# Delta rule of a two-block model: key products and M three units ahead, neighbouring units' work between the dependent products, and no identity products

## The reference, cut to what matters

```
gc = cumsum(g);  decay[i,j] = exp(gc_i - gc_j) for i >= j
m    = strict_lower((k*beta) @ k.T * decay)         # "M"
tmat = inverse(I + m)                               # triangular
u    = tmat @ (v*beta);  w = tmat @ (k*beta*exp(gc))
qk   = (q @ k.T) * decay
# over the chunks, with a state s (64 x 64 per head):
v_new = u - w @ s
o     = (q*exp(gc)) @ s + qk @ v_new
s     = s * g_last + k_dec.T @ v_new
```

## Time and profile before

| | us |
|---|---|
| median of 3 runs (lowest, highest) | 3595.54 (3592.28, 3597.2) |
| the profiled execution: its own time | 3594.88 |
| its span, first to last instruction | 3593.1 |
| PE busy in the span | 3366.4 (94%) |
| PE weight loads busy | 2497.4 (70%) |
| DVE, ACT, POOL busy | 1653.8, 1210.2, 1035.1 |
| first transpose of unit 0 in `gdn`, first product of the next stage | 1772.03, 2095.78 |

### The profile page before, as it was taken

How to read it: one execution, slowest core, us unless ns; L and a number is a source line. 1 busy time by engine, 2 the same in 40 slices (tenths; PEclk the granted TensorE clock), 3 DMA queues, 4 the chain that set the end, 5 groups by cost and what they waited for, 6 DMA issues and landing times.

```text
span 3593.1 us, 43314 instructions
## 1 busy us (share of the span) xinstructions
PE 3366.4 (94%) x17748; PEld 2497.4 (70%) x17748; DVE 1653.8 (46%) x3116; ACT 1210.2 (34%) x2188; POOL 1035.1 (29%) x894
## 2 busy tenths in 40 slices
PE   7999999888899999989799998999999998999998
PEld 3346888655788865645588866888887547848886
DVE  7744446598466666224455524112224117721213
ACT  2413333347323336135422214212213226733222
POOL 0233444460344410021244402222222022014443
PEclk9999999999999999999999899999999999999999
DMA  7424555210355541100111111111111112012222
GB/s 295 186 93 153 209 200 199 88 47 1 117 200 209 213 181 47 46 27 1 33 47 38 29 60 46 71 70 49 71 69 49 53 38 74 1 47 94 95 104 83
DMA packets 67621, 335.56 MB, mean 93 GB/s; under 512 B 32416, under 2 KB 35424, under 8 KB 42592
## 3 DMA queue, kind: packets, MB, share of 16 engines
q1 hardware_dynamic: 66560, 330.56, 24.6%
q10 hardware_dynamic: 864, 2.24, 0.2%
HBM read 325.86 MB, written 6.91 MB: 93 GB/s over the span
## 4 chain that ended last, share of the span: by engine, by line
PE 77%; DVE 11%; ACT 5%; DMA 2%; POOL 2%; issue 2%; SPq 1%; POOLq 0%; DVEq 0%; ACTq 0%
PE PSB L557 15%; PE PSB L649 14%; PE PSB L653 14%; PE PSB L650 14%; PE PSB L1235 2%; PE PSB L1257 2%; PE PSB L1244 2%; PE PSB L3006 1%; DVE SB L390 1%; DMA SB<-in_ada 1%; PE PSB L1796 1%; DVE SB L1329 1%; DVE SB L1640 1%; DVE SB L1345 1%; DVE SB L1638 1%
## 5 line engine op out<-in xcount | busy, mean ns | idle before, releaser
L653 PE MATMUL PSB<-R,WSR 128*128 128x512 f32 x2556 | 871.9, 371 | 0.0
L557 PE MATMUL PSB<-SB 128*128 128x512 f32 x1760 | 655.2, 534 | 11.8 <-ACT SB L1455 9.2
L623 POOL TENSOR_TENSOR WSR<-SB,ahead 128x1024 fp32r<-128x1024 f32 x164 | 393.1, 2397 | 672.8 <-ACT ahead L592 672.8
L557 PEld LDWEIGHTS PSB<-SB 128*128 128x128 f32 x1760 | 338.8, 193 | 325.6 <-issue 299.5
L649 PE MATMUL PSB<-R,ahead 128*128 128x512 f32 x1528 | 561.9, 368 | 0.0
L650 PE MATMUL PSB<-R,ahead 128*128 128x512 f32 x1528 | 546.1, 367 | 0.0
L653 PEld LDWEIGHTS PSB<-R,WSR 128*128 128x128 f32 x2556 | 449.6, 189 | 64.1
L623 POOL TENSOR_TENSOR WSR<-SB,ffn_weights 128x1024 fp32r<-128x1024 f32 x96 | 230.2, 2398 | 389.9 <-ACT ffn_weights L592 389.9
L649 PEld LDWEIGHTS PSB<-R,ahead 128*128 128x128 f32 x1528 | 286.9, 188 | 63.1
L649 PE MATMUL PSB<-R,ffn_weights 128*128 128x512 f32 x868 | 324.4, 374 | 6.3 <-POOL WSR L623 6.2
L650 PEld LDWEIGHTS PSB<-R,ahead 128*128 128x128 f32 x1528 | 287.0, 188 | 48.3
(11 more groups left out here) (377 smaller groups left out, 4839.7 us busy)
## 6 DMA issues: line engine op xcount, KB each, us to landing
SB<-in_w SPq DMA_DIRECT2D x95, 2048.0 KB, 8.2
SB<-in_ada SPq DMA_DIRECT2D x96, 1024.0 KB, 5.2
SB<-gate_rows SPq DMA_DIRECT2D x12, 512.0 KB, 3.9
SB<-in_rpb SPq DMA_DIRECT2D x8, 448.0 KB, 3.6
spill<-SB SPq DMA_DIRECT2D x1, 3072.0 KB, 9.6
SB<-gate_rows SPq DMA_DIRECT2D x24, 128.0 KB, 3.8
SB<-spill SPq DMA_DIRECT2D x1, 3072.0 KB, 11.5
SB<-in_x SPq DMA_DIRECT2D x8, 256.0 KB, 6.5
```

What stands on the lines that cost most here:

```text
L557: ins = e.mm(banks[ring[(g + c) % len(ring)]][0:m, 0:n], t[:, 0:m], xs[k][:, lo:lo + n], k == 0, k == nkt - 1)
L623: e.tt(lr, t, hf, ALU.subtract).then_inc(*G.up(("lo", j)))
L653: ins = e.mm(b[:, 0:n], wl, xh[:, lo:lo + n], False, last)
```

## The change

- The identity products are gone: every count in `BUSY` is 0.
- `kk` and the decay are made three units ahead (`kk(n + 3)`, `decay(n + 3)`, `products(n + 3)`). M and the decay get a third buffer. Its place is one of the two slots of the weight panels; the panel that was loaded into it early is now loaded near the end of the stage, after level 6's first product of unit 9.
- s and o of unit n - 1 move from the end of unit n - 1 to just behind the transposes of unit n (for units 9 and later they stay at the end of the unit). The tokens, `kq` and the DVE work on them are for unit n + 1 in place of n + 2, and stand between the levels; so do both parts of `past`. `carried` now stands behind `products` on DVE.
- SP issues `blocks_sp(n + 3)` ahead of `inverse_sp(n + 2)`. POOL clears DT for n + 1, inverts n + 2, then adds the output of n - 1, then takes the past off the values of n + 1.

```diff
-BUSY = {("y", 4): 4, ("d", 4): 2, ("y", 5): 2, ("d", 5): 4, ("y", 6): 5, ("u", 6): 1}
+BUSY = {("y", 4): lambda n: 0, ("d", 4): lambda n: 0,
+        ("y", 5): lambda n: 0, ("d", 5): lambda n: 0,
+        ("y", 6): lambda n: 0, ("u", 6): lambda n: 0}
 FF2 = ((0, 4), (4, 8), (8, 12), (12, 16), (16, 19), (19, 22))
...
-            MTd, DMd, DTd = ([XREG[:, i * 2048 + d * 1024:i * 2048 + (d + 1) * 1024] for d in range(2)] for i in range(3))
-            DM, DT, MT = ([a[d][:, y * 512:(y + 1) * 512] for d in range(2) for y in range(2)] for a in (DMd, DTd, MTd))
-            dec = lambda n: DECAY[n % 2]
+            late = W.where["e_out", 0, 0] // PANEL
+            spare = wslot[(late + 1) % NSLOT]
+            MTn, DMd, DTd = ([XREG[:, i * 2048 + d * 1024:i * 2048 + (d + 1) * 1024] for d in range(2)] for i in range(3))
+            MTn = [spare[:, 0:1024]] + MTn
+            DECAY = [spare[:, 1024:2048]] + DECAY
+            DM, DT = ([a[d][:, y * 512:(y + 1) * 512] for d in range(2) for y in range(2)] for a in (DMd, DTd))
+            mt_of = lambda n: MTn[n % 3]
+            dec = lambda n: DECAY[n % 3]
...
+                if 1 <= n < 10:
+                    use(n - 1, "s"), use(n - 1, "o")
+                use(n, "y", 0, 4), use(n, "y", 1, 4)
+                if 1 <= n < 11:
+                    use(n + 1, "vq", 0)
+                use(n, "d", 0, 4), use(n, "d", 1, 4)
+                use_front(n + 1, ("tok", 0), ("tok", 1))
+                use(n, "y", 0, 5), use(n, "y", 1, 5)
+                use(n, "t", 0, 4), use(n, "t", 1, 4)
+                if n == 11:
+                    use("out", 4)
+                use_front(n + 1, ("kq", 0), ("kq", 1))
+                use(n, "d", 0, 5), use(n, "d", 1, 5)
+                if 1 <= n < 11:
+                    use(n + 1, "vq", 1)
+                use(n, "y", 0, 6), use(n, "y", 1, 6)
+                use_front(n + 3, ("kk", 0), ("kk", 1))
...
             def front_sp(e):
 
-                panels(e, "e_out", 0, 0)
                 e.wait_ge(rows_out, 32)
                 e.wait_ge(*mst.at("q_turn", 7))
+                e.wait_ge(*mst.at("panel", late - 1))
                 gates_in(e, 0)
-                e.wait_ge(*mst.at("score", 35))
                 gates_in(e, 1)
+                gates_in(e, 2)
                 blocks_sp(e, 0)
                 inverse_sp(e, 0)
 
             def sp(e):
                 after(e, st)
-                for n in range(12):
-                    if n < 10:
-                        gates_in(e, n + 2)
-                    if n < 11:
-                        blocks_sp(e, n + 1)
-                        inverse_sp(e, n + 1)
+                blocks_sp(e, 1)
+                gates_in(e, 3)
+                inverse_sp(e, 1)
+                blocks_sp(e, 2)
+                for n in range(10):
+                    if n < 8:
+                        gates_in(e, n + 4)
+                    if n < 9:
+                        blocks_sp(e, n + 3)
+                    inverse_sp(e, n + 2)
+                e.wait_ge(*st.at("md", 9, 1, 6))
+                e.wait_ge(*st.at("at", 9, 1))
+                panels(e, "e_out", 0, 0)
 
             def gates_in(e, n):
                 d, c, cl, j0 = chunk(n)
                 u = 2 * c + d
                 if n >= 2:
-                    e.wait_ge(*st.at("at", n - 2, 1))
-                    e.wait_ge(*st.at("mt", n - 2, 1))
+                    e.wait_ge(*st.at("kk", n - 2, 1))
+                if n >= 3:
+                    e.wait_ge(*st.at("at", n - 3, 1))
+                    e.wait_ge(*st.at("mt", n - 3, 1))
...
+                    if 1 <= n < 10:
+                        state(n - 1)
+                        out_of(n - 1)
...
                     doubled(4)
                     past(n + 1, 0)
                     corrected(4)
-                    past(n + 1, 1)
+                    tokens(n + 1, 0), tokens(n + 1, 1)
                     doubled(5)
                     turned(4)
                     if n == 11:
                         out(4)
+                    kq(n + 1)
                     corrected(5)
+                    past(n + 1, 1)
                     for y in range(2):
...
-                    kk(n + 2)
+                    kk(n + 3)
                     turned(5)
...
-                    kq(n + 2)
-                    tokens(n + 2, 0)
+                    if n == 9:
+                        state(n)
                     if n == 11:
                         out(2), out(1)
-                    e.wait_ge(*st.at("u", n))
-                    if n < 10:
-                        free(e, n, "s")
-                        e.wait_ge(*st.at("kd", n))
-                        for h in range(8):
-                            e.mm(bank(n, "s")[par(h % 2), col(h // 2, 64)], KD[d][:, col(h, 64)], U[d][:, col(h, 64)]).then_inc(*P.up(("s_sum", n)))
-                    free(e, n, "o")
-                    e.wait_ge(*st.at("at", n, 0))
-                    e.wait_ge(*st.at("at", n, 1))
-                    for h in range(8):
-                        e.mm(bank(n, "o")[:, col(h, 64)], AT[d][:, col(h)], U[d][:, col(h, 64)]).then_inc(*P.up(("o_sum", n)))
-                    tokens(n + 2, 1)
+                    if n >= 9:
+                        out_of(n)
...
+                    if 1 <= n < 10:
+                        state(n - 1)
+                    decay_arg(n + 3)
...
-                        if lv == 5:
-                            carried(n + 1)
+                        if lv == 5 and n < 11:
+                            values(n + 1), keys(n + 1)
+                        if lv == 4 and 1 <= n < 10:
+                            out_of(n - 1)
...
-                    products(n + 2, 0)
-                    products(n + 2, 1)
+                    scores(n + 1, 0), scores(n + 1, 1)
+                    products(n + 3, 0), products(n + 3, 1)
+                    carried(n + 1)
...
+                def added(n):
+                    c = chunk(n)[1]
+                    e.wait_ge(*st.at("o", n))
+                    e.wait_ge(*st.at("o_zero", c))
+                    if n:
+                        e.wait_ge(*st.at("o_added", n - 1))
+                    e.tt(O[c], O[c], TQ[n % 2], ALU.add).then_inc(*G.up(("o_added", n)))
+
+                cleared_pool(e, 1)
+                inverse(1)
                 for n in range(12):
-                    d, c, cl, j0 = chunk(n)
-                    inverse(n + 1)
+                    d = n % 2
+                    if n:
+                        cleared_pool(e, n + 1)
+                    inverse(n + 2)
+                    if 1 <= n < 10:
+                        added(n - 1)
                     if 1 <= n < 11:
                         e.wait_ge(*st.at("past", n + 1))
                         e.wait_ge(*st.at("vb", n + 1))
                         e.tt(VB[1 - d], VB[1 - d], U[1 - d], ALU.subtract).then_inc(*G.up(("rest", n + 1)))
-                    e.wait_ge(*st.at("o", n))
-                    e.wait_ge(*st.at("o_zero", c))
-                    if n:
-                        e.wait_ge(*st.at("o_added", n - 1))
-                    e.tt(O[c], O[c], TQ[d], ALU.add).then_inc(*G.up(("o_added", n)))
+                    if n >= 9:
+                        added(n)
```

More of the change, by code:

```diff
@@ L2032, in mla, with first_out @@
             tb = att.tbanks
+            def first_out(tile_):
+                return min(NSLOT, W.where["e_out", 0, 0] // PANEL + 1 - W.where[tile_] // PANEL)
             def sp(e):
@@ L2397, in pe, with out_of, state @@
                 after(e, st)
-                for n in range(2):
-                    if n:
-                        kk(n)
-                    kq(n), tokens(n, 0), tokens(n, 1)
+                def out_of(n):
+                    d = n % 2
+                    free(e, n, "o")
+                    e.wait_ge(*st.at("u", n))
+                    e.wait_ge(*st.at("at", n, 0))
+                    e.wait_ge(*st.at("at", n, 1))
+                    for h in range(8):
+                        e.mm(bank(n, "o")[:, col(h, 64)], AT[d][:, col(h)], U[d][:, col(h, 64)]).then_inc(*P.up(("o_sum", n)))
+                def state(n):
+                    d = n % 2
+                    free(e, n, "s")
+                    e.wait_ge(*st.at("u", n))
+                    e.wait_ge(*st.at("kd", n))
+                    for h in range(8):
+                        e.mm(bank(n, "s")[par(h % 2), col(h // 2, 64)], KD[d][:, col(h, 64)], U[d][:, col(h, 64)]).then_inc(*P.up(("s_sum", n)))
+                kk(1)
+                kq(0), tokens(0, 0), tokens(0, 1)
+                kk(2)
                 for n in range(12):
@@ L2665, in dve, with state, out_of @@
                     v.memset(SS[d], 0.0).then_inc(*D.up())
-                for n in range(2):
-                    if n:
-                        products(n, 0), products(n, 1)
-                    scores(n, 0), keys(n), scores(n, 1), values(n)
+                def state(n):
+                    d, c, cl, j0 = chunk(n)
```

(43 more changed lines are left out.)

70 lines of the change are left out of this document (32 added, 38 removed).

## The result

| | before | changed |
|---|---|---|
| median of 20 runs (lowest, highest), us | 3597.51 (3590.91, 3604.38) | 3606.40 (3597.94, 3618.39) |
| profiled execution: its own time, span | 3594.88, 3593.1 | 3600.53, 3598.7 |
| mean granted clock of that execution | 0.973 | 0.961 |
| T0 to T2, T2 to T10, T10 to the end of the stage, us | 54.0, 212.2, 57.5 | 59.9, 207.3, 60.0 |

The account below looks back on a forecast made before the run. Two rounds of about 25.8 us a unit, SP-POOL-transfers and PE, were taken to bind. Units -27.7, start +5 and +1.5, end -1, clock +12 gave -10.2: profiled 3584.7, median 3585.4; range 3571 to 3605.

Parts of the forecast that it names:

- the one of a unit at full clock: Sign of being right: transposes 22 to 24 us apart in units 2 to 8 where PEclk is 1.0.
- one of being wrong: Sign of being wrong: the first product of the next stage starts no earlier than 2095.8.
- a unit without a fall: PE's dependent steps in one steady unit at full clock: sum 22.8 us against 25.8, bounds 22.3 and 24.
- T2 to T10 without falls: From unit 2's transposes to unit 10's, before clock losses: 184.5 us, 27.7 less than before.
- falls in these eight units: PE's clock drops in units 2 to 9: four at 3 us each, +12, bounds +0 and +35.
- start, to T2: Up to unit 2's transposes: +5 from POOL's two inverses before added(0), +1.5 from low clock; bounds +1 and +10.
- units 10 and 11: Stage's last two units: chains of waits, -1 together for identity products at low clock; bounds -2.5 and +2.
- the price of a fall: Cost of one clock drop behind level 6: 3 us, against 4.4 read from unit 7 of the kernel before.
- The slower one: Rival: the clock falls in every unit, eight falls costing 35 us, +13 in all, 3608; chance 0.15.
- The first rival: Rival: the clock falls no more often than before, so the 12 goes: -22, 3573; chance 0.24.
- POOL as the bound of every unit: Rival: added behind the inverse holds up carried in every unit, units back at 25.8: +2, 3597; chance 0.14.
- the one weighed ahead: Skill's rule on PE's clock: avoid long idle gaps between bursts; by it alone no steady unit would fall.

Follow-up runs that it names:

- e2: Changed kernel with three identity products a unit, only in level 6: one ahead of its second product, two ahead of u; 3587.08 us, ratio 0.9973.
- e5: e2 with the start mended: unit 3's decay taken up later in unit 0, POOL adding output n - 1 before inverse n + 2; 3576.70 us, 0.9941.
- e10: e2 with only POOL's order changed: output of n - 1 added ahead of the inverse of n + 2; 3576.12 us, ratio 0.9937.
- e6: e5 with the identity product counts of the kernel before put back ahead of the levels in units 10 and 11; 3578.01 us, 0.9943.
- e3: Kernel before with all 18 identity products a unit taken out, nothing else changed; 3650.28 us, ratio 1.0151.
- e11: Kernel before with 8 identity products a unit, in level 6 alone (5, 1 and 2), those of levels 4 and 5 gone; 3600.82 us, 1.0005.
- e12: e8 with keys(n + 1) on DVE behind level 4's subtraction in place of behind level 5's mask; 3562.36 us, ratio 0.9901.
- e7: Changed kernel with three identity products a unit, ahead of level 4's second and both of level 5's products; 3608.00 us, ratio 1.0030.
- e8: e6 with kk(n + 3) moved between level 6's second product and u, replacing identity products there in units 0 to 8; 3571.07 us, 0.9925.
- e9: e2 with only the decay of unit 3 taken up later in unit 0; 3586.44 us, ratio 0.9974.

## Why the prediction was wrong

The forecast was 3585.4; the measured 3606.4 is just above the range's 3605. Of the signs named ahead, the one of a unit at full clock came (22.8 us), and so did one of being wrong: the next stage's first product starts at 2101.2, no earlier than 2095.8. In the profiled execution, step by step:

| step | predicted | measured |
|---|---|---|
| a unit without a fall | 22.8 | 22.8 (e2, e5) |
| T2 to T10 without falls | 184.5 | 184.6 (e5), 184.5 (e10) |
| falls in these eight units | 4 x 3 = 12 | 4 x 5.7 = 22.8 |
| start, to T2 | +5 +1.5 | +5.9 |
| units 10 and 11 | -1 | +2.5 |
| the stage | -10.2 | +3.4 |

**The failed step** is the price of a fall: "I expect four in the eight units from 2 to 9, at 3 us each, fewer than 4.4 because kq and tokens no longer stand in the slow stretch". The number of falls was right, but by luck: no step of the prediction gives four and not some other number. Each took 5.7 us: two units next to each other are 23.9 + 27.4 = 51.3 for 2 x 22.8 = 45.6. Two things made 3 of it.

First, the old price was read too low. I took 4.4 from unit 7 alone, but the low stretch goes on into unit 8, whose row and first two PE rows are these (kernel before; warm they take 1.04 and 1.13):

```profile
1986.00:2012.60 26.60, 25.84 (x327) 23.66 (x326) 15.02 (x25) 7.04 (x17) 12.31 (x35) 0.93 0.19 42
```

```profile
1986.02 1.91 PE L2411 MATMUL PSB<-SB 128*128 128x128 f32 x8
1987.73 1.91 PE L2417 MATMUL PSB<-SB 128*128 128x128 f32 x8
```

Both units together are 30.2 + 26.6 = 56.8 us for 2 x 25.8 = 51.6: the fall cost 5.2, nearly what one costs in the new order. Second, I took 1.4 off for the steps that leave the slow stretch, as if the stretch ended with them. It lasted about 14 us in both kernels, so what leaves is replaced by what comes next, and here that is the chain itself. The prediction priced u, o and the transposes (0.6, 1.8 and 0.9 by its rows; 1.09, 1.68 and 0.88 came); s, level 4's two products and the key part of `past` stood in the slow stretch too and took 0.43, 0.83, 0.45 and 0.92 more. Of the 2.7 us by which the price was short, 0.8 is the reading of unit 7 alone, 1.4 is what I took off and 0.5 is the new order. 22.8 for 12 is 10.8 of the 13.6 us by which the stage missed.

**The rest of the stage.** The end explains another 3.5; the start gives back 0.6. The end's term was argued from identity products at low clock, and e6 shows that they had no say there.

**From the stage to the medians.** Of the 8.9 us, the profiled executions show 5.65: 3.4 in this stage, 2.0 ahead of it and 0.2 behind it. Ahead of it a difference of 2.3 is there already at the first head's projection, where nothing was changed and which differs from execution to execution. The other 3.2 lie in executions without a trace. Their mean granted clocks are listed: of the changed kernel's 20 runs, the fastest (3597.94) has 0.963, the three slowest (3616.93 to 3618.39) 0.957, 0.954 and 0.956; the profiled one, at 3600.53, has 0.961 and is the third fastest. That the clock falls more often in the slower ones is what these numbers fit; no trace shows where.

**The rivals.** The slower one had the right mechanism, the clock, and its 3608 is near the result, but for another reason than its sum: not eight falls at 4.4 from a sixth on, but four at 5.7, a later end, and what the untraced executions add. The first rival (no more falls, 3573) is nearest to e10 and e5, 3576.1 and 3576.7, but these have the start mended as well; e2, with the start as it was, came to 3587.1. POOL as the bound of every unit did not come: SP's waits for POOL are gone, and units at full clock take 22.8. Its +2 does not come out of the prediction's own numbers either: eight units of 25.8, +6.5 and -1 make -0.3.

**The start** came out as sized, 5.9 us for 6.5, but not as told, and that is luck too. I had put a gap of about 10 us on PE in unit 1, ended by the last subtraction. In the changed kernel's profile unit 1 has no PE gap over 0.67 us and DVE does not wait for POOL in it; the surplus is in unit 0, behind the wait for gate rows, which I had not seen coming. The mechanism I had named, `added(0)` behind the inverse of unit 3, shows only where the clock is kept (4.08 us in e2), and there it is what e10 removes.

**What I said of the identity products**, "worth nothing by themselves: they stood before waits", was wrong as to their worth. As work they were free where they stood; as clock they were worth 53 us to the kernel before (e3), and 8 of them in level 6 bring all of that back (e11).

The Trainium skill has a rule beside the one weighed ahead, in "TensorE: Matmul & The Clock Gate", under "A second HAM failure mode": frequent short idle times between groups of matmuls let the clock go back and forth, at a cost in throughput. The changed kernel agrees that it needs no long gap, since the idle times ahead of a fall are 0.34 and 0.60 us. But short gaps alone don't tell it: e12 keeps gaps of 0.50, 0.53 and 0.37 us in its levels and stays at 1.00, and e7 has as many gaps filled as e2 and falls.

## What to carry to other kernels

Work that looks like mere filler may be what holds the clock: before taking it out, or moving real work past it, ask which stretch of small products with gaps it stands in, and keep something there, best of all work that must be done anyway (e8). Price a fall of the clock by the steps that the whole slow stretch will cover in the new order, and read what one costs over all the units that it touches, not over the one in which it starts. And where two waits follow each other, test each alone: the longer one may only be hiding the later (e9, e10).

## What the runs showed of the hardware

The busy share of PE does not tell a unit that loses its clock from one that keeps it: 21.88 of 25.60 us are busy at PEclk 1.00 in e11, 20.88 of 23.90, a larger share, in the changed kernel's unit at whose end the clock falls. Three identity products can do it or not: in e7 the clock falls in some units, in e2 from unit 3 to unit 9 in none. What e2 has at the place that matters is one of 0.39 us ahead of level 6's second product and two of 0.71 together ahead of u. And low stretches last about 14 us in the kernel before and in the changed one (in e3 longer: PEclk 0.70 over 34.10 us), though PE works in them almost without a gap (24.82 of 27.40 us busy in the slow unit), and in the changed kernel they lie in units 3, 5, 7 and 9, not in every one. Why every second, and what exactly the chip measures, these runs leave open.
